# Gathering a pair of experts in two halves, with the repairs of a first neighbour

## The chip, the core and the metric

The kernel runs on one core of one Trainium2 chip. The metric is the device time of one execution, in microseconds (us). All products are on TensorE (PE); ScalarE (ACT), VectorE (DVE) and GpSimd (POOL) prepare operands and handle results, and SyncE (SP) issues the loads.

## The reference, cut to what matters

256 rows of width 1024 in fp32 go through two layers, the second with eight experts, and through a further block. What the change touches:

```python
h = h + g1 * attention(...)                                # layers 0 and 1
h = h + g2 * ffn(rms_norm(h, g) * (1 + sc2) + sh2)         # layer 0: SwiGLU; layer 1: 8 experts, top 2
# each expert: y = (silu(x @ w1) * (x @ w3)) @ w2, w1 and w3 1024x1408, w2 1408x1024

proj = rms_norm(h) @ w_in                                  # second block
qkv_a, q_c, kv_c, k_pe, gates = split(proj)                # gates = sigmoid(... + b_gate)
o_a = mixer_dilated(qkv_a, pos) @ w_o_a                    # below: a2
q, kv = rms_norm(q_c) @ w_uq, rms_norm(kv_c) @ w_ukv
o_b = mixer_mla(q, kv, rotary(k_pe), pos) @ w_o_b          # below: a3
h = h + rms_norm((g_a * o_a + g_b * o_b) @ w_out)
h = h + rms_norm(square(relu(rms_norm(h) @ w_ff1)) @ w_ff2)
```

## The kernel before, in words

**Products.** A fp32 product is three matmuls of rounded halves (`mm3`, L930 to L932): low by high, high by low, high by high. A weight tile of at most 128x2048 is loaded to `raw` by a queue of SP, ACT copies it rounded to `whi` (L1566), DVE subtracts to get `wlo` (L2133), and PE may then use it. The name of a tile's slot recurs: `whi__62` and `wlo__61` belong to `raw__60`, and so on in pairs; the same slot holds a new tile every few products.

**Order.** Each engine's program is written out by hand, one function per engine. At many places of ACT's and DVE's programs stands `feed(event)`: it converts there every tile that PE uses up to `at["ahead"]` tiles behind the tile in use at that event of PE's program. So where PE's event is placed moves the conversions in ACT's and DVE's order.

**PSUM banks.** `take(ring, ...)` gives PE the next bank of a ring and waits for what emptied that bank's last holder. Ring "8" goes round all eight banks (`turn_of["8"]` is its position), "o" is banks 6 and 7, "c" is 4 and 5, "x" is 0 to 3. Who waits for whom thus depends on the ring's position.

**Layer 0's feed-forward norm ("f").** Four row tiles are squared (`norm_square`), scaled (`norm_scale`), turned by PE (`norm_turn`) and split in halves (`norm_turned`), between tiles of the first product.

**Experts** (PE: `experts`, `hidden`, `turn_hidden`, `scatter`, `gather`). For each of eight experts: two products x by w1 and w3 in three chunks of columns (tiles of 128x2048, 128x1536 for the last chunk), each chunk turned, then the output product with w2 in six tiles, k0 = 0, 2, ..., 10 (the last of 128x1024). The scatter of expert ex-1 follows the first chunk of ex. The rows of two experts are gathered together by matmuls with a selection matrix: four turns of 128x128 ("gp", L936), then four pieces "gx" of eight matmuls (L1364), at k0 = 4 of the odd experts 1, 3 and 5. ACT and DVE scale the pieces (L1907, L2935), ACT rounds them (`pair_hi`, L1621), DVE subtracts (`moe__217`, L2205). `scattered` on DVE adds into MACC (`moe__211`, `moe__212`, L2978), for the last expert into the residual h_t (`keep__50`); the output product of that expert is multiplied by the gate row in its bank (L3013, `output_lo`) before ACT and DVE split it. POOL multiplies MACC by the gate row (L3387) and adds it to h_t (L3390), in two pairs of 128x1024 behind expert 6's scatter.

**Second block.** `norm_turn("s", 0)`, then six projections s0 to s5 and two of the latent vectors, lat0 and lat1 (`proj`, two banks each). Heads of each are turned while the next is multiplied. `gates` gives the gate projection in four parts on banks 4 and 5 (ring "c"): the first part is run at once (`advance(fill, 16)`), lat1's heads are turned, and the others fill a2's attention. Behind a2 come the products uq, ukv, their turns "mqt" (L936) and attention a3 (`attend("a3")`: scores L1182, `TENSOR_REDUCE` L2427, exponent L1645, value product L1210), in which the two tiles of the next product are converted (`at["ahead"]` is 2 from step lag + 3 on), then the output products, a norm and the MLP.

## Time and profile before

| | |
|---|---|
| median of 3 runs | 1799.89 us (1798.51 to 1800.46) |
| the profiled execution | 1800.71 us, its span 1798.5 us |
| PE busy | 1669.8 us, 93% |
| DVE busy | 1239.5 us, 69% |
| ACT busy | 832.8 us, 46% |
| POOL busy | 144.8 us, 8% |

The profiled execution is 2.2 us longer than its span, which starts with the first instruction and ends with the last; times at which something happens count from the span's start. The bracket at the end of a timeline row is the time that the engine stood idle before that instruction, and what ended it. A granted clock of 1.00 is TensorE's 2.4 GHz, 0.50 is 1.2 GHz.

### The profile page before, as it was taken

The page shows a single profiled execution, that of the slowest core. Times are in us where ns is not written, and L with a number is a line of the kernel's source. Part 1 is how long each engine was busy: PE and PEld are TensorE (multiplying, and loading weights), DVE is VectorE, ACT ScalarE, POOL GpSimd, SP SyncE. Part 2 cuts the span into 40 slices and gives each one's busy share as a digit, 9 for nine tenths or more (in the row PEclk, how much of TensorE's full clock was granted, in tenths as well). Part 3 has the DMA queues.
Part 4 walks back from the last instruction along what each step waited for, and adds up shares of the span by engine and source line. Part 5 has one row for each costly group of instructions (what it writes and reads, how often), then busy time and mean ns, then how long its engine had stood idle before and what let it go on. Part 6 is the DMA issues. An engine that isn't in the chain of part 4 may idle for free. (4 is left out here: it accounts for less than half of the span.)

```text
span 1798.5 us, 21440 instructions
## 1 busy us (share of the span) xinstructions
PE 1669.8 (93%) x8686; PEld 1423.7 (79%) x8686; DVE 1239.5 (69%) x1618; ACT 832.8 (46%) x1015; POOL 144.8 (8%) x152
## 2 busy tenths in 40 slices
PE   5999988999999998798799999999989788989998
PEld 3778877888888887797688788887779667779986
DVE  6578854587565536767689898889976465566643
ACT  6354433322122325334467677667654334545532
POOL 2110102000110022310100000000300000000000
PEclk9999989999999998998799999999999899889999
DMA  8344423355565422211479898988865422135553
GB/s 338 96 164 133 155 90 116 141 197 195 205 257 187 173 68 94 71 48 48 164 256 345 298 359 326 335 325 321 324 216 179 141 82 94 65 135 187 188 187 117
DMA packets 60504, 333.60 MB, mean 185 GB/s; under 512 B 14690, under 2 KB 15009, under 8 KB 28400
## 3 DMA queue, kind: packets, MB, share of 16 engines
q1 hardware_dynamic: 54640, 311.06, 47.6%
q0 software_dynamic: 4032, 14.57, 2.6%
q10 hardware_dynamic: 1728, 6.54, 1.0%
q8 instruction: 72, 1.18, 0.3%
q14 instruction: 32, 0.26, 0.0%
HBM read 331.00 MB, written 1.13 MB: 185 GB/s over the span
## 5 line engine op out<-in xcount | busy, mean ns | idle before, releaser
L2133 DVE TENSOR_TENSOR wlo__61<-raw__60,whi__62 128x2048 fp32r<-128x2048 f32 (+2 forms) x64 | 145.2, 2269 | 72.7 <-ACT whi__62 L1566 72.5
L2133 DVE TENSOR_TENSOR wlo__65<-raw__64,whi__66 128x2048 fp32r<-128x2048 f32 (+3 forms) x64 | 141.1, 2204 | 73.2 <-ACT whi__66 L1566 73.2
L1566 ACT ACTIVATE whi__62<-raw__60 128x2048 fp32r<-128x2048 f32 (+2 forms) x64 | 118.9, 1858 | 88.9 <-DMA raw__60<-in_ffn_w 42.4
L1566 ACT ACTIVATE whi__66<-raw__64 128x2048 fp32r<-128x2048 f32 (+3 forms) x64 | 115.3, 1802 | 82.2 <-DMA raw__64<-in_ffn_w 29.5
L2133 DVE TENSOR_TENSOR wlo__69<-raw__68,whi__70 128x2048 fp32r<-128x2048 f32 (+4 forms) x50 | 109.2, 2185 | 31.0 <-ACT whi__70 L1566 30.9
L2169 DVE SCALAR_TENSOR_TENSOR wsum__71<-raw__68,silu_rows 128x1024 f32<-128x1024 f32 x84 | 99.9, 1219 | 1.4 <-DMA raw__68<-in_ada_w 0.9
L3297 POOL TENSOR_TENSOR keep__58<-keep__58,keep__59 128x1 f32<-128x1 f32 (+3 forms) x48 | 51.6, 1079 | 593.4 <-DVE keep__58 L2210 593.3
L1566 ACT ACTIVATE whi__70<-raw__68 128x2048 fp32r<-128x2048 f32 (+4 forms) x50 | 90.4, 1808 | 15.8 <-DMA raw__68<-in_w_ff 11.6
L2133 DVE TENSOR_TENSOR wlo__235<-raw__234,whi__236 128x2048 fp32r<-128x2048 f32 (+1 forms) x24 | 50.6, 2110 | 11.8 <-ACT whi__236 L1566 11.8
L2427 DVE TENSOR_REDUCE keep__58<-ps 128x1 f32<-128x256 f32 (+1 forms) x88 | 44.5, 517 | 18.5 <-PE ps L1182 9.9
L2133 DVE TENSOR_TENSOR wlo__231<-raw__230,whi__232 128x2048 fp32r<-128x2048 f32 (+1 forms) x24 | 52.7, 2197 | 0.0
L930 PE MATMUL ps<-ffn__129,wlo__61 128*128 128x512 f32 (+1 forms) x128 | 47.7, 372 | 4.7 <-DVE ffn__130 L2205 2.9
L931 PE MATMUL ps<-ffn__130,whi__62 128*128 128x512 f32 (+1 forms) x128 | 47.1, 368 | 0.0
L932 PE MATMUL ps<-ffn__129,whi__62 128*128 128x512 f32 (+1 forms) x128 | 47.0, 367 | 0.0
L1566 ACT ACTIVATE whi__232<-raw__230 128x2048 fp32r<-128x2048 f32 (+1 forms) x24 | 42.4, 1768 | 9.6 <-DMA raw__230<-in_moe_w 9.5
L930 PE MATMUL ps<-ffn__129,wlo__141 128*128 128x512 f32 x112 | 43.6, 389 | 0.0
L931 PE MATMUL ps<-ffn__130,whi__142 128*128 128x512 f32 x112 | 43.6, 389 | 0.0
L932 PE MATMUL ps<-ffn__129,whi__142 128*128 128x512 f32 x112 | 43.6, 389 | 0.0
L930 PE MATMUL ps<-ffn__129,wlo__65 128*128 128x512 f32 x112 | 43.6, 389 | 0.0
L931 PE MATMUL ps<-ffn__130,whi__66 128*128 128x512 f32 x112 | 43.6, 389 | 0.0
L932 PE MATMUL ps<-ffn__129,whi__66 128*128 128x512 f32 x112 | 43.6, 389 | 0.0
L2169 DVE SCALAR_TENSOR_TENSOR wsum__147<-raw__144,silu_rows 128x1024 f32<-128x1024 f32 x36 | 43.2, 1220 | 0.5
(1169 smaller groups left out, 5326.9 us busy)
## 6 DMA issues: line engine op xcount, KB each, us to landing
raw__68<-in_moe_w SPq DMA_DIRECT2D x24, 1024.0 KB, 5.0
raw__60<-in_moe_w SPq DMA_DIRECT2D x24, 1024.0 KB, 5.4
raw__68<-in_ada_w SPq DMA_DIRECT2D x16, 1024.0 KB, 4.9
raw__64<-in_moe_w SPq DMA_DIRECT2D x16, 1024.0 KB, 5.2
raw__230<-in_moe_w SPq DMA_DIRECT2D x16, 1024.0 KB, 5.9
raw__234<-in_moe_w SPq DMA_DIRECT2D x16, 1024.0 KB, 6.4
raw__144<-in_ada_w SPq DMA_DIRECT2D x13, 1024.0 KB, 6.2
raw__68<-in_ada_w POOLq DMA_DIRECT2D x20, 512.0 KB, 4.1
```

The source lines that it names most:

```text
L930: e.matmul(out, ll, rh, start=start, stop=False)
L931: e.matmul(out, lh, rl, start=False, stop=False)
L932: return e.matmul(out, lh, rh, start=False, stop=stop)
L1566: e.activation(t.hi(), t.raw(), ACT.Copy).then_inc(*did("hi", i))
L2133: e.tensor_tensor(t.lo(), t.raw(), t.hi().bitcast(F32), ALU.subtract).then_inc(*did("lo", i))
L2169: m = e.scalar_tensor_tensor(out=junk, in0=slot_raw[t.slot][:, c * 1024:c * 1024 + 1024], scalar=1.0, in1=CB[:, v * D:(v + 1) * D], op0=AL ...
L2427: m = e.tensor_reduce(neg, b[:, 0:u.total], AX.X, ALU.max, negate=True)
L3297: e.tensor_tensor(x, x, EXPO[:, 0:1].broadcast_to([128, n_]) if n_ > 1 else EXPO[:, 0:1], ALU.pow).then_inc(*did(out, *key))
```

## The change

Five edits. (1) The gather of an odd expert's next pair is split: "gp" and the first two pieces stand behind k0 = 2, the other two behind k0 = 4. (2) Expert 6's output is treated as expert 7's was: multiplied by the gate row in its bank, split, and added straight into h_t; POOL's two pairs of 128x1024 become four of 128x512, released one by one by four events of experts 5 and 6. (3) In the second block ring "8" is no longer set to position 6: s0 takes banks 6 and 7 from ring "o", and the ring is moved on by two. (4) In a3 one tile is converted at step lag + 2 on ACT and lag + 4 on DVE, the other five steps later. (5) In layer 0's norm "f" one `feed` stands ahead of `norm_square(3)` on ACT and `norm_scale(3)` on DVE.

```diff
@@ -1346,3 +1346,3 @@
 
-        def gather(r, p):
+        def gather_turn(r, p):
             b = take("8", "gp", r, p)
@@ -1355,3 +1355,5 @@
             m.then_inc(*done("gp", r, p))
-            for kb in range(4):
+
+        def gather(r, p, pieces):
+            for kb in pieces:
                 b = take("8", "gx", r, p, kb)
@@ -1367,3 +1369,2 @@
                 m.then_inc(*done("gx", r, p, kb))
-            turn_of["8"] += 2
 
@@ -1410,3 +1411,5 @@
         def experts(r):
-            gather(r, 0)
+            gather_turn(r, 0)
+            gather(r, 0, range(4))
+            turn_of["8"] += 2
             for ex in range(8):
@@ -1432,6 +1435,11 @@
                     consumed(tile, "y", r, ex, k0)
-                    if k0 == 4 and ex % 2 and ex < 7:
-                        gather(r, (ex + 1) // 2)
                     if k0 == 2:
                         turn_hidden(r, ex, 2)
+                    if ex % 2 and ex < 7:
+                        if k0 == 2:
+                            gather_turn(r, (ex + 1) // 2)
+                            gather(r, (ex + 1) // 2, range(0, 2))
+                        elif k0 == 4:
+                            gather(r, (ex + 1) // 2, range(2, 4))
+                            turn_of["8"] += 2
                 if not r and ex == 1:
@@ -1468,3 +1476,2 @@
         norm_turn("s", 0)
-        turn_of["8"] += -turn_of["8"] % 8 + 6
         w_in = W["w_in_2"]
@@ -1474,3 +1481,5 @@
                 lent[slot_s] = [("scat", 1, 7, 1, 1)]
-            proj(("s", n), x4(AT2s), 2, KT, w_in[:, n * 384:(n + 1) * 384], 384, rdy("s"))
+            proj(("s", n), x4(AT2s), 2, KT, w_in[:, n * 384:(n + 1) * 384], 384, rdy("s"), "8" if n else "o")
+            if n == 0:
+                turn_of["8"] += 2
             if 0 < n < 5:
@@ -1630,5 +1639,5 @@
             A = HEADS[st]
+            if st == "a3":
+                at["ahead"] = 0
             for i in A.steps():
-                if st == "a3":
-                    at["ahead"] = 2 if i > A.lag + 2 else 0
                 if st == "a0":
@@ -1678,2 +1687,6 @@
                         e.activation(XT[1], bank("o", st, u.group), ACT.Square).then_inc(*did("hsq", "fin", u.group))
+                if st == "a3" and i - A.lag in (2, 7):
+                    at["ahead"] = 1 + (i - A.lag) // 7
+                    feed(("score", st, i, 0))
+                    at["ahead"] -= i - A.lag == 2
                 j = i - A.lag - 3
@@ -1788,3 +1801,7 @@
             norm_turned(N, 0)
-            at["ahead"] = 1 if N == "o" else 2
+            if N == "o":
+                at["ahead"] = 1
+            else:
+                at["ahead"] = 2
+                feed(("nt", N, 0, 6))
             norm_square(N, 3)
@@ -1957,3 +1974,3 @@
                 high("yph", (r, ex, half), YP[0][:, half * 512:half * 512 + 512], bank("y", r, ex, half),
-                     *([("yg", r, ex, half)] if r or ex == 7 else [("y", r, ex, 10)]), *xg_free(r, ex, "scat", 1, 1))
+                     *([("yg", r, ex, half)] if r or ex > 5 else [("y", r, ex, 10)]), *xg_free(r, ex, "scat", 1, 1))
 
@@ -2398,5 +2415,5 @@
             A = HEADS[st]
+            if st == "a3":
+                at["ahead"] = 0
             for i in A.steps():
-                if st == "a3":
-                    at["ahead"] = 2 if i > A.lag + 2 else 0
                 if st == "a0":
@@ -2466,2 +2483,6 @@
                     finished(st, A.units[j], j)
+                if st == "a3" and i - A.lag in (4, 9):
+                    at["ahead"] = 1 + (i - A.lag) // 9
+                    feed(("score", st, i, 0))
+                    at["ahead"] -= i - A.lag == 4
                 j = i - A.lag - 3
@@ -2628,2 +2649,3 @@
         at["ahead"] = 2
+        feed(("nt", "f", 0, 6))
         norm_scale("f", 3)
@@ -2940,3 +2962,3 @@
                     split_more(4, ("gx", r, p, kb))
-                for piece in (0,) if kb == 0 else (1, 2, 3):
+                for piece in ((0,), (1, 2, 3))[kb // 2] if p == 0 else (kb, kb + 1):
                     pair = slice(piece * 2, piece * 2 + 2)
@@ -2969,4 +2991,4 @@
                     past = [("acc", r, ex - 1, t, half)] if ex else [("acc", 0, 7, t, half)] if r else []
-                    past = past + ([("hpre", t)] if (r, ex) == (0, 7) else [])
-                    if r or ex == 7:
+                    past = past + ([("hpre", t, half)] if (r, ex) == (0, 6) else [])
+                    if r or ex > 5:
                         dst = h_t[t][:, half * 512:half * 512 + 512]
@@ -3008,3 +3030,3 @@
         def output_lo(r, ex):
-            for half in range(2) if r or ex == 7 else ():
+            for half in range(2) if r or ex > 5 else ():
                 for s, n in due(("y", r, ex, 10), *spr(11)):
@@ -3384,8 +3406,11 @@
         for t in range(2):
-            for s, n in due(("acc", 0, 6, t, 0), ("acc", 0, 6, t, 1), *spr(11)):
-                e.wait_ge(s, n)
-            e.tensor_tensor(MACC[t], MACC[t], GBC[:, D:2 * D], ALU.mult).then_inc(*did("hgate", t))
-            for s, n in due(("hgate", t)):
-                e.wait_ge(s, n)
-            e.tensor_tensor(h_t[t], h_t[t], MACC[t], ALU.add).then_inc(*did("hpre", t))
+            for half in range(2):
+                hs, gs = (slice(o + half * 512, o + half * 512 + 512) for o in (0, D))
+                pace = [("acc", 0, 5, 1, 1), ("hid", 0, 6, 2, 4, "3"), ("y", 0, 6, 2), ("y", 0, 6, 6)][2 * t + half]
+                for s, n in due(("acc", 0, 5, t, half), pace, *spr(11)):
+                    e.wait_ge(s, n)
+                e.tensor_tensor(MACC[t][:, hs], MACC[t][:, hs], GBC[:, gs], ALU.mult).then_inc(*did("hgate", t, half))
+                for s, n in due(("hgate", t, half)):
+                    e.wait_ge(s, n)
+                e.tensor_tensor(h_t[t][:, hs], h_t[t][:, hs], MACC[t][:, hs], ALU.add).then_inc(*did("hpre", t, half))
         for t in range(2):
```

ACT's order at the gather of expert 3, before (`whi11__236` is the tile of k0 = 8, `moe22__219` a scaled piece, `pair_hi_216` a rounded one, `whi12__240` the tile of k0 = 10):

```order
L1566 ACTIVATE whi11__236<-raw11__234 128x2048 [waits s_raw11]
L1898 ACTIVATE moe30__227<-ps3 128x512 [waits s_slot_in]
L1907 ACTIVATE moe22__219<-ps5,keep4__52 128x256 [waits s_slot_in]
L1907 ACTIVATE moe22__219<-ps5,keep4__52 128x256
L1621 ACTIVATE pair_hi_216<-moe21__218 128x512 [waits s_hid,s_moe_v]
L1621 ACTIVATE pair_hi_216<-moe22__219 128x512 [waits s_moe_a]
L1621 ACTIVATE pair_hi_216<-moe21__218 128x512 [waits s_moe_v]
L1907 ACTIVATE moe22__219<-ps7,keep4__52 128x256 [waits s_moe_v,s_slot_in]
L1907 ACTIVATE moe22__219<-ps7,keep4__52 128x256
L1621 ACTIVATE pair_hi_216<-moe22__219 128x512 [waits s_moe_a]
L1566 ACTIVATE whi12__240<-raw12__238 128x1024 [waits s_raw12]
L1566 ACTIVATE whi2__70<-raw2__68 128x2048 [waits s_raw2]
```

and in the change:

```order
L1915 ACTIVATE moe30__227<-ps3 128x512 [waits s_slot_in]
L1924 ACTIVATE moe22__219<-ps5,keep4__52 128x256 [waits s_slot_in]
L1924 ACTIVATE moe22__219<-ps5,keep4__52 128x256
L1630 ACTIVATE pair_hi_216<-moe21__218 128x512 [waits s_hid,s_moe_v]
L1630 ACTIVATE pair_hi_216<-moe22__219 128x512 [waits s_moe_a]
L1575 ACTIVATE whi11__236<-raw11__234 128x2048 [waits s_raw11]
L1630 ACTIVATE pair_hi_216<-moe21__218 128x512 [waits s_moe_v]
L1924 ACTIVATE moe22__219<-ps7,keep4__52 128x256 [waits s_slot_in]
L1924 ACTIVATE moe22__219<-ps7,keep4__52 128x256
L1630 ACTIVATE pair_hi_216<-moe22__219 128x512 [waits s_moe_a]
L1575 ACTIVATE whi12__240<-raw12__238 128x1024 [waits s_raw12]
L1575 ACTIVATE whi2__70<-raw2__68 128x2048 [waits s_raw2]
```

The tile of k0 = 8 stood ahead of all pieces, and stands between the second and the third. On DVE `wlo__235` moves in the same way, behind the second subtraction. PE's order of the pieces, and their banks, are as before.

PE at the head turns of lat0 and at the first matmul of the gates, before:

```order
L936 MATMUL ps0<-keep1__49,mix14__257 128x128 [waits s_mix_v]
L936 MATMUL ps0<-keep1__49,mix14__257 128x128 x3
L936 MATMUL ps1<-keep1__49,mix12__255 128x128 [waits s_mix_v,s_mix_a]
L936 MATMUL ps1<-keep1__49,mix12__255 128x128 x3
L930 MATMUL ps4<-whi0__62,mix20__267 128x512 [waits s_hi,s_lo,s_mix_v]
L931 MATMUL ps4<-wlo0__61,mix19__266 128x512
L932 MATMUL ps4<-whi0__62,mix19__266 128x512
```

and in the change:

```order
L936 MATMUL ps0<-keep1__49,mix14__257 128x128 [waits s_mix_v]
L936 MATMUL ps0<-keep1__49,mix14__257 128x128 x3
L936 MATMUL ps1<-keep1__49,mix12__255 128x128 [waits s_mix_v]
L936 MATMUL ps1<-keep1__49,mix12__255 128x128 x3
L930 MATMUL ps4<-whi0__62,mix20__267 128x512 [waits s_lo,s_hi]
L931 MATMUL ps4<-wlo0__61,mix19__266 128x512
L932 MATMUL ps4<-whi0__62,mix19__266 128x512
```

The gates' first bank was last held by lat1, and its matmul waited for DVE (s_mix_v) to empty it. Now lat1 is in banks 6 and 7 and lat0 in 4 and 5, and the matmul has no wait for DVE's results. In the same way uq's first matmul moves from bank 6, with a wait for s_att_v, to bank 0, without it.

DVE in a3, before (`TENSOR_REDUCE` is one step's maximum of the scores):

```order
L2462 COPY mix36__283<-ps4 128x256 [waits s_turn]
L2427 TENSOR_REDUCE keep10__58<-ps0 128x1 [waits s_score]
L2427 TENSOR_REDUCE keep10__58<-ps2 128x1 [waits s_score]
L2462 COPY mix36__283<-ps3 128x256 [waits s_pv,s_turn]
L2133 TENSOR_TENSOR wlo0__61<-raw0__60,whi0__62 128x1024 [waits s_hi]
L2133 TENSOR_TENSOR wlo1__65<-raw1__64,whi1__66 128x1024 [waits s_hi]
L2427 TENSOR_REDUCE keep10__58<-ps4 128x1 [waits s_score]
L2427 TENSOR_REDUCE keep10__58<-ps1 128x1 [waits s_score]
L2462 COPY mix36__283<-ps2 128x256 [waits s_pv,s_turn]
```

and in the change:

```order
L2479 COPY mix36__283<-ps4 128x256 [waits s_turn]
L2444 TENSOR_REDUCE keep10__58<-ps0 128x1 [waits s_score]
L2444 TENSOR_REDUCE keep10__58<-ps2 128x1 [waits s_score]
L2479 COPY mix36__283<-ps3 128x256 [waits s_pv,s_turn]
L2444 TENSOR_REDUCE keep10__58<-ps4 128x1 [waits s_score]
L2444 TENSOR_REDUCE keep10__58<-ps1 128x1 [waits s_score]
L2479 COPY mix36__283<-ps2 128x256 [waits s_pv,s_turn]
L2150 TENSOR_TENSOR wlo0__61<-raw0__60,whi0__62 128x1024 [waits s_hi]
L2444 TENSOR_REDUCE keep10__58<-ps3 128x1 [waits s_score]
L2444 TENSOR_REDUCE keep10__58<-ps0 128x1 [waits s_score]
```

Two conversions in a row stood behind two reductions of this stretch; now the first stands alone behind four, and the second (`wlo1__65`) comes eight rows further on.

## Rows read from the trace of the kernel before

**Rows 1.** PE's waits: waited for, us in total, times, longest.

```profile
PE ps L930 <- ACT moe__228 L1621: 4.0, 3, 1.3
...
PE ps L930 <- DVE wlo__239 L2133: 2.3, 3, 0.8
```

**Rows 2.** Windows: us, busy by engine, then PE's granted clock, DMA share, GB/s.

```profile
314.40:318.20 3.80, 3.73 (x18) 3.76 (x19) 0.00 (x0) 0.00 (x0) 0.00 (x0) 0.55 0.00 0
...
1415.80:1420.60 4.80, 4.71 (x11) 3.75 (x12) 2.19 (x1) 0.92 (x1) 0.00 (x0) 0.51 0.00 0
...
1508.00:1512.70 4.70, 4.69 (x15) 4.70 (x16) 1.23 (x1) 3.02 (x3) 0.00 (x0) 0.51 0.00 0
...
1538.00:1553.00 15.00, 14.73 (x63) 12.91 (x64) 5.55 (x13) 5.48 (x19) 0.00 (x0) 0.56 0.01 2
```

**Rows 3.** Timeline around the gates: start us, us, engine, line, instruction, [idle before].

```profile
1405.79 2.29 DVE L2133 TENSOR_TENSOR wlo__65<-raw__64,whi__66 128x2048 fp32r<-128x2048 f32 x1 [1.85 <-ACT whi__66 L1566]
...
1415.25 0.54 DVE L3113 TENSOR_SCALAR mix__257<-ps,keep__58 128x256 f32<-128x256 f32 x1 [0.67 <-POOL keep__58 L3297]
...
1415.89 0.76 PE L930 MATMUL ps<-whi__62,mix__267 128*128 128x512 f32 x1 [9.66 <-DVE mix__257 L3113]
...
1429.05 0.38 PE L936 MATMUL ps<-keep__49,mix__256 128*128 128x128 f32 x2
```

**Rows 4.** Timeline behind a2, DVE, PE and ACT.

```profile
1507.33 0.42 DVE L2386 TENSOR_TENSOR mix__286<-mix__286,mix__256 128x256 f32<-128x256 f32 x1
...
1508.01 0.66 PE L930 MATMUL ps<-whi__62,mix__251 128*128 128x384 f32 x1 [4.28 <-ACT mix__245 L2042]
...
1509.51 1.04 ACT L1566 ACTIVATE whi__264<-raw__262 128x1024 fp32r<-128x1024 f32 x1
```

**Rows 5.** Timeline in a3, DVE and PE.

```profile
1534.64 1.23 DVE L2133 TENSOR_TENSOR wlo__61<-raw__60,whi__62 128x1024 fp32r<-128x1024 f32 x1 [1.25 <-ACT whi__62 L1566]
...
1536.92 0.75 DVE L2427 TENSOR_REDUCE keep__58<-ps 128x1 f32<-128x256 f32 x2
...
1538.27 0.66 PE L1210 MATMUL ps<-mix__249,mix__284 128*128 128x64 f32 x4 [3.06 <-ACT mix__284 L1657]
```

**Rows 6.** Timeline in layer 0's norm, ACT and PE.

```profile
307.05 1.05 ACT L1572 ACTIVATE ffn__134<-keep__50 128x1024 f32<-128x1024 f32 x1
...
310.10 1.90 ACT L1566 ACTIVATE whi__70<-raw__68 128x2048 fp32r<-128x2048 f32 x1
...
314.47 0.46 PE L930 MATMUL ps<-ffn__129,wlo__69 128*128 128x256 f32 x1 [2.42 <-DVE wlo__69 L2133]
```

**Rows 7.** Timeline at the gather of expert 1, PE, DVE and ACT.

```profile
993.01 0.49 PE L936 MATMUL ps<-keep__49,moe__223 128*128 128x128 f32 x3
...
996.50 0.36 PE L1364 MATMUL ps<-moe__214,moe__198 128*128 128x256 f32 x1
...
998.08 0.99 DVE L2935 TENSOR_SCALAR moe__218<-ps,keep__52 128x256 f32<-128x256 f32 x2
...
1000.30 0.28 PE L1364 MATMUL ps<-moe__215,moe__199 128*128 128x256 f32 x1
...
1003.81 0.63 ACT L1621 ACTIVATE pair_hi<-moe__219 128x512 fp32r<-128x512 f32 x1
...
1009.75 0.46 PE L930 MATMUL ps<-whi__70,moe__217 128*128 128x512 f32 x1 [1.33 <-ACT moe__228 L1621]
```

**Rows 8.** Windows in experts 6 and 7.

```profile
1250.00:1275.00 25.00, 25.00 (x117) 20.83 (x117) 22.71 (x16) 19.17 (x15) 0.00 (x0) 1.00 0.98 365
...
1283.00:1303.00 20.00, 16.19 (x75) 12.81 (x74) 20.00 (x10) 10.83 (x9) 14.94 (x4) 1.00 0.75 266
```

**Rows 9.** Timeline, POOL beside DVE, and expert 6's end on DVE.

```profile
655.41 1.29 POOL L3307 TENSOR_TENSOR keep__50<-keep__50,ffn__148 128x512 f32<-128x512 f32 x1 [4.59 <-DVE ffn__148 L2476]
...
1272.12 2.29 DVE L2133 TENSOR_TENSOR wlo__65<-raw__64,whi__66 128x2048 fp32r<-128x2048 f32 x1 [0.38 <-ACT whi__66 L1566]
...
1287.50 4.49 DVE L2133 TENSOR_TENSOR wlo__61<-raw__60,whi__62 128x2048 fp32r<-128x2048 f32 x1
```

## The prediction

> **What bounds the kernel.** The shares come first: PE is busy 93% of the span, so an edit pays if it removes idle time of PE or time at which PE runs at 1.2 GHz. PE's waits by releaser tell which idle time the five edits can reach. The largest has its own row in the timeline: the gates' first matmul, 9.66 us [rows 3]. Next are uq's, 4.28 us [rows 4], a3's, 3.06 us [rows 5], the norm's, 2.42 us [rows 6], and two of about 0.8 and 1.3 us at each of the gathers of experts 1, 3 and 5, together 6.3 us [rows 1]. The windows then tell what follows such a gap: behind four of them the granted clock is about half [rows 2], while it is full in the experts [rows 8]. In a window, one minus the clock, times its length, is what 1.2 GHz cost, if PE would have been busy anyway.
>
> **Gather in two halves: +0.7 us at each of three places, +2 in all.** No matmul is added, and the matmuls of the gather were on PE's path before and stay there. What limits the next expert is the chain on ACT and DVE: last piece rounded, tile of k0 = 10 converted, then the next expert's first tile, for which PE waits until 1009.75 [rows 7] (the row names `moe__228` on ACT, but that had long been done; it is `wlo__69`). The last rounding ends at 1004.44 (1003.81 + 0.63) [rows 7]. In the change the first half follows the turn of the third chunk, which starts at 993.01 and takes 0.4 on the array; the 32 gather matmuls start 0.12 us apart (996.50 to 1000.30) [rows 7], so four turns and 16 of them take 2.4 and two pieces have left PE at 995.8. From there, an instruction that follows another starting 0.1 us before the rows' duration is over: 0.95 for scaling two half pieces, 1.1 for two roundings [rows 7], 1.8 for ACT's copy `whi__236` that now stands here [rows 6], 2.2 for `wlo__235` [rows 9], 0.95 for scaling the third piece, which waits on DVE behind that, 0.6 for its rounding, 0.95 and 0.6 for the fourth: 9.15, so 1004.95, and with semaphores between engines, of a few hundredths each, 1005.1, or 0.7 later than before. The earlier start is used up by a conversion of 4.0 us that stood ahead of the pieces and now stands between them. Behind it the chain is as before, and the next tiles are paced by DVE too, so PE doesn't get it back. Bounds: all 6.3 us of waits gone; or 1 us lost at each.
>
> **Expert 6 and the repairs: +1.7 us.** Beside POOL's four instructions PE idles 3.8 us of 20 (16.19 busy) [rows 8], since a conversion on DVE takes 4.49 us [rows 9] and not 2.29 as at 1272.12 [rows 9]. That is the gain: expert 7 has no POOL beside it, -3.8. Now the same POOL work lies in expert 6. A POOL instruction of 128x512 alone takes 1.29 us [rows 9]; I take it that each blocks one conversion for 1.15 us, half of the 2.2 us by which 4.49 exceeds 2.29. The first pair falls where DVE is well ahead and costs nothing: its cover is the slack of the tiles behind the scatter, and without it it would cost up to 2.3. The other three pairs fall into the output product: six times 1.15 is 6.9 us on DVE. To it the two multiplications of expert 6's output add 1.3, and ACT's rounding, queued behind them, delays `whi__66`, for which `wlo__65` already waited 0.38 us [rows 9]: 0.5 more. Of these 8.7 us, 2.3 fit into DVE's idle time there (22.71 busy of 25) [rows 8], while PE has none, and 0.9 into the lead that DVE has at the end of it: +5.5 for PE. Net +1.7. Bounds: nothing of it on PE, -3.8; or +4. DVE's additions for expert 6 change their target only, and POOL's last pair ends some 10 us before they need it.
> How the two engines share is a choice. I let them take turns, each POOL instruction stopping the next conversion. If both ran at half speed while both work, the same 7 us would fall on DVE sooner, some of it on tiles with less slack, and I make it +2.4; the row of 4.49 us [rows 9] fits either. The Trainium skill, page "SBUF — State Buffer", section "Who interferes with whom", speaks for turns: it calls the port pair of Vector and GpSimd an exclusive lock, which a Vector instruction with two SBUF inputs can run into. By that rule the term is +1.7, by the other reading +2.4; no row here decides.
>
> **Bank rotation: -11.7 and -6.4 us.** Nothing is added; what goes is two waits for banks. PE could begin the gates as soon as the heads of lat0 are turned, 9.66 us sooner [rows 3]. Their first tile was ready then, their second at 1408.08 (1405.79 + 2.29) [rows 3], before it is needed. The window behind the gap has clock 0.51 over 4.8 us [rows 2]: 2.35 more. Lat1's heads were turned at 1429.05 and would be at 1417.0, and DVE has them by 1415.8 (1415.25 + 0.54) [rows 3]: no new wait, but only 1.2 us to spare. I take 11.7 of the 12.0. The second wait is put down to ACT's sigmoid, but uq needs nothing of it: its bank was emptied by DVE at 1507.75 (1507.33 + 0.42) [rows 4], just before it started. So 4.28 and (1 - 0.51) x 4.7 = 2.3 go [rows 2, 4]: 6.6. Late next is ukv's tile: `whi__264` stays behind the sigmoids until 1510.55, `wlo` takes 1.2 more [rows 4, 5], so 1511.8; ukv would start at about 1512.0. I take 6.4. Bounds for both together: the gaps alone, -13.9, or less by what is given back, and -18.6.
>
> **Tiles of a3: -5.5 us.** Two conversions of 1.2 us stood ahead of a step's reduction at 1536.92, for which PE waited 3.06 us [rows 5]. With one behind two more reductions I leave a gap of 1 us: -2. The clock of 0.56 over 15 us cost 6.6 us at most [rows 2], and without the gap need not fall; but at 2.4 GHz ACT and DVE pace part of these steps, so I take 3.5, about half. Bounds: -1 (half clock comes anyway) and -8.
>
> **Norm of layer 0: -3.5 us.** ACT's copy `whi__70` stood behind square and scale of the fourth row tile, from 307.05 to 310.10 [rows 6]. First in line, it and `wlo__69` are done 3 us sooner, and PE's 2.42 us [rows 6] go with (1 - 0.55) x 3.8 = 1.7 at half clock [rows 2]: 4.1 at most. The norm's fourth tile comes 2 to 3 us later, and PE turns it some 5 us after the gap: its cover, and without it the gap would only move there. Bounds: -2 and -4.1.
>
> **Sum:** 2 + 1.7 - 18.1 - 5.5 - 3.5 = -23.4. The profiled execution took 1800.71 us (2.2 outside its span), which would become 1777.3; the median of the runs is 0.8 lower, 1799.89, so I forecast 1776.5.
>
> **Rivals.**
> (a) The gaps go and the half clock stays, or comes at other gaps close by. Then 2.35 + 2.3 + 3.5 + 1.3 = 9.4 are not gained: 1786. For it: a3 and the norm keep smaller gaps. Against: in the rows it always follows a long gap.
> (b) Gather and repairs do what one would hope: the pieces are ready early, the 6.3 us of waits go, and DVE hides the repairs (-3.8). That is 13.8 better than my sum: 1763. For it: PE delivers the first two pieces about 3 us sooner. Against: the order on ACT and the busy DVE above. Half of it, 1770, is likelier than all.
> (c) a2's steps, paced by ACT and DVE, give back the gates' gain: 1776.5 + 11.7 = 1788. For it: DVE has only 1.2 us to spare ahead of a2. Against: a2's tiles and heads were ready long before.
> (d) The change doesn't do what it says at uq: the wait really is for the sigmoid, as its row has it. Then 6.4 stay: 1783. Against: no operand or bank of uq comes from it.
> (e) Slower: turning the ring by two gives s1 to s5 the wait that the gates had, for the banks of heads not yet turned and emptied. Five such waits of 9.66 us would be 48, and 1825 the time; from 4.7 us each on, the change is slower. For it: nothing but the ring's position made the gates wait. Against: PE's order shows no new wait at these five.
>
> **From this to the numbers.** My forecast 0.52, (a) 0.15, (b) 0.17 with its half, (c) 0.07, (d) 0.05, (e) 0.02, no effect of the large edits for some cause that I don't see 0.02. The range 1766 to 1788 leaves out (e), the last, the full (b) and the ends of (a) and (c). About 0.2%, 3.6 us, is what a measurement of this kernel can tell from no change. Faster by more 0.95, within it 0.02, slower by more 0.03, where (e) is joined by the outer end of sums of bounds.
>
> **What would show it.** Right: the gates' first matmul at once behind lat0's turns, at full clock; a2's first score some 12 us sooner relative to s5; uq without a gap and ukv close behind its tile; a gap of about 1 us in a3 and clock 1.00 behind it; no wait for `wlo__69` in layer 0's norm; at three gathers the waits for `wlo__239` and the next tile a bit longer than before; PE's idle time moved from expert 7 to the end of expert 6. Wrong: the waits at the gathers shorter than before, an expert 6 without waits, half clock in a3, or a new gap in a2 of several us.

## The result, and the profile after

The change takes 1770.27 us (median of four runs, 1768.70 to 1772.38), where the kernel before took 1799.70 beside it: 0.984 of its time, interval 0.982 to 0.986, or 29.4 us less. Forecast were 1776.5 and 23.4 less; the time lies in the range.

The page of the change (busy time, share of the span, instructions; then the clock in tenths of full speed, in 40 slices):

```profile
PE 1651.8 (94%) x8686; PEld 1407.3 (80%) x8686; DVE 1236.6 (70%) x1620; ACT 831.4 (47%) x1015; POOL 155.7 (9%) x156
...
PEclk9999989999999999898889999999999999999999
```

PE has the same 8686 matmuls and is busy for 18.0 us less (1669.8 before): they run longer at 1.2 GHz, and less time is spent there. The remainder is idle time. PE's waits (us in all, times, longest):

```profile
PE ps L930 <- DVE wlo__239 L2150: 4.6, 3, 1.6
...
PE ps L930 <- DVE wlo__65 L2150: 4.4, 3, 2.9
...
PE ps L930 <- ACT moe__228 L1630: 3.9, 3, 1.3
```

The wait for `wlo__239` at the gathers has doubled, that for the next tile is as before [rows 1], and one of 2.9 us for `wlo__65` is new. Against it stand waits that are gone: the gates', uq's, the norm's and the four of expert 7; a3's is cut into smaller ones. Cut by PE's first use of a tile, the two profiled executions compare as follows (us):

| stretch | before | after | change | forecast |
|---|---|---|---|---|
| up to layer 0's norm, untouched | 304.8 | 302.0 | -2.8 | 0 |
| norm | 67.3 | 62.3 | -4.9 | -3.5 |
| up to the first split gather, untouched | 628.6 | 627.3 | -1.3 | 0 |
| three gathers and their experts | 216.6 | 218.9 | +2.4 | +2.1 |
| expert 6 and 7 | 85.8 | 86.1 | +0.3 (+5.2, -4.9) | +1.7 (+5.5, -3.8) |
| up to s5 | 37.7 | 37.2 | -0.5 | 0 |
| gates | 91.6 | 80.1 | -11.6 | -11.7 |
| a2 and uq | 82.3 | 75.7 | -6.5 | -6.4 |
| a3 | 44.8 | 37.9 | -6.8 | -5.5 |

The sum is -31.7; -27.6 of it is where the edits are or behind them, and 4.1 is in stretches whose order is unchanged. Half clock, below, is a granted clock of 0.50, 1.2 GHz.

The gates, their second head turn, the first score of a2, and uq, on PE:

```profile
1398.71 0.60 PE L936 MATMUL ps<-keep__49,mix__255 128*128 128x128 f32 x4
1399.06 0.47 PE L930 MATMUL ps<-whi__62,mix__267 128*128 128x512 f32 x1
...
1412.16 0.70 PE L1182 MATMUL ps<-mix__248,keep__50 128*128 128x256 f32 x2 [1.50 <-DVE mix__257 L3090]
...
1485.12 0.42 PE L930 MATMUL ps<-whi__62,mix__251 128*128 128x384 f32 x1
```

Of the 9.66 us [rows 3] and 4.28 us [rows 4] nothing is left; in front of a2's first score PE waits 1.50 us, where it was 1.00 before. The windows over these places, over a3 and over the norm (us, busy by engine, granted clock, DMA share, GB/s):

```profile
1399.00:1411.00 12.00, 11.66 (x55) 9.47 (x53) 9.27 (x19) 5.78 (x8) 1.10 (x2) 1.00 0.65 252
1504.00:1526.00 22.00, 19.85 (x132) 16.33 (x130) 13.17 (x30) 14.12 (x44) 0.00 (x0) 1.00 0.00 1
306.00:312.00 6.00, 6.00 (x53) 6.00 (x52) 2.36 (x2) 2.37 (x4) 0.55 (x1) 1.00 0.25 104
1485.00:1492.00 7.00, 7.00 (x43) 7.00 (x43) 3.37 (x13) 6.02 (x5) 0.00 (x0) 1.00 0.20 71
```

Where 0.51 to 0.56 stood [rows 2], the clock is 1.00. In a3 PE's waits for `mix__284` are four of 0.16, 0.34, 0.42 and 0.86 us now, where it was one of 3.06 [rows 5]. The two conversions of a3 [rows 5] on DVE, now 6.9 us apart:

```profile
1510.75 1.22 DVE L2150 TENSOR_TENSOR wlo__61<-raw__60,whi__62 128x1024 fp32r<-128x1024 f32 x1
...
1517.63 1.21 DVE L2150 TENSOR_TENSOR wlo__65<-raw__64,whi__66 128x1024 fp32r<-128x1024 f32 x1
```

In the norm, ACT's copy comes first, and PE has no gap in front of the first tile's products that use `wlo__69` [rows 6]:

```profile
304.27 1.90 ACT L1575 ACTIVATE whi__70<-raw__68 128x2048 fp32r<-128x2048 f32 x1
...
309.11 0.28 PE L930 MATMUL ps<-ffn__129,wlo__69 128*128 128x256 f32 x1
```

### The profile page after: what moved, and what is told of

It is laid out like the page before. It is cut to its first block and busy times, and to the rows that moved or that the text cites. A ratio compares the mean times of both kernels' runs of the same rounds, so it can differ in the third digit from the quotient of the medians.

```text
span 1766.6 us, 21439 instructions
## 1 busy us (share of the span) xinstructions
PE 1651.8 (94%) x8686; PEld 1407.3 (80%) x8686; DVE 1236.6 (70%) x1620; ACT 831.4 (47%) x1015; POOL 155.7 (9%) x156
## 5 line engine op out<-in xcount | busy, mean ns | idle before, releaser
L2150 DVE TENSOR_TENSOR wlo__61<-raw__60,whi__62 128x2048 fp32r<-128x2048 f32 (+2 forms) x64 | 144.2, 2253 | 72.9 <-ACT whi__62 L1575 72.7
L2186 DVE SCALAR_TENSOR_TENSOR wsum__71<-raw__68,silu_rows 128x1024 f32<-128x1024 f32 x84 | 100.0, 1221 | 1.2 <-DMA raw__68<-in_ada_w 0.6
L2150 DVE TENSOR_TENSOR wlo__239<-raw__238,whi__240 128x2048 fp32r<-128x2048 f32 (+2 forms) x24 | 43.2, 1800 | 0.9 <-ACT whi__240 L1575 0.8
```

Of the source, the lines that this page charges most:

```text
L2150: e.tensor_tensor(t.lo(), t.raw(), t.hi().bitcast(F32), ALU.subtract).then_inc(*did("lo", i))
L2186: m = e.scalar_tensor_tensor(out=junk, in0=slot_raw[t.slot][:, c * 1024:c * 1024 + 1024], scalar=1.0, in1=CB[:, v * D:(v + 1) * D], op0=AL ...
```

## The experiments

Twelve kernels were run in three sets, each beside the kernel before on the same chip (its medians were 1800.46, 1799.83 and 1799.43 us, nine runs each). `whole`, `tile_first`, `ring_only` and `old_repairs` ran on one chip, the other eight, `change_again` among them, on a second. Diffs are against the change unless another base is named. None of the kernels leaves out a part of the computation.

### The gather: what splitting it costs

**`whole`** undoes the split alone.

```diff
+                    if k0 == 4 and ex % 2 and ex < 7:
+                        gather_turn(r, (ex + 1) // 2)
+                        gather(r, (ex + 1) // 2, range(4))
+                        turn_of["8"] += 2
...
-                for piece in ((0,), (1, 2, 3))[kb // 2] if p == 0 else (kb, kb + 1):
+                for piece in (0,) if kb == 0 else (1, 2, 3):
```

> The changed kernel with its first edit undone: the gather of a pair stands whole behind k0 = 4, all else as in the change. Theory 1 (the tile of k0 = 8, converted between the two halves, delays the last piece by 0.8 us at each of three gathers): the waits ahead of the tile of k0 = 10 fall from 1.5 to 0.75 us, the three together give back 2.4 us, so 1768 where the change has 1770.3. Rival (the split saves as much elsewhere as it loses, or the delay at the gathers is made good in the next expert): 1770 within 1, or above.

It took 1768.11 us (0.983 of before, 0.982 to 0.984). PE at the first gather of this kernel:

```profile
1001.23 0.47 PE L930 MATMUL ps<-whi__240,moe__225 128*128 128x512 f32 x1 [0.77 <-DVE wlo__239 L2147]
...
1004.16 0.47 PE L930 MATMUL ps<-whi__70,moe__217 128*128 128x512 f32 x1 [1.29 <-ACT moe__228 L1627]
```

and of the change (ACT's and DVE's conversion of the tile of k0 = 8, DVE's scaling of the third piece, then PE):

```profile
988.84 1.91 ACT L1575 ACTIVATE whi__236<-raw__234 128x2048 fp32r<-128x2048 f32 x1
...
990.78 2.29 DVE L2150 TENSOR_TENSOR wlo__235<-raw__234,whi__236 128x2048 fp32r<-128x2048 f32 x1 [1.03 <-ACT whi__236 L1575]
992.99 0.99 DVE L2957 TENSOR_SCALAR moe__218<-ps,keep__52 128x256 f32<-128x256 f32 x2
...
998.57 0.47 PE L930 MATMUL ps<-whi__240,moe__225 128*128 128x512 f32 x1 [1.55 <-DVE wlo__239 L2150]
...
1001.50 0.47 PE L930 MATMUL ps<-whi__70,moe__217 128*128 128x512 f32 x1 [1.30 <-ACT moe__228 L1630]
```

The wait for `wlo__239` is 1.55 with the split and 0.77 without it; the next is the same. The rows above it show the chain of the prediction: ACT's conversion at 988.84 and DVE's at 990.78 now stand between the second and the third piece, whose scaling starts at 992.99. Each of the three gathers is some 0.77 us longer than in `whole`, 2.3 in all; +2.1 were forecast. The medians differ by 2.2 us with intervals that overlap, so it is the traces that show it: the edit that names the change slows it.

**`tile_first`** keeps the split and puts the tile of k0 = 8 ahead of the pieces again. On ACT `at["ahead"] += p > 0` stands around `feed(("gp", r, p))`; on DVE:

```diff
+                if p and kb == 0:
+                    at["ahead"] += 1
+                    feed(("gx", r, p, kb))
+                    at["ahead"] -= 1
                 for piece in ((0,), (1, 2, 3))[kb // 2] if p == 0 else (kb, kb + 1):
```

> The changed kernel, gather in two halves as there, but the tile of k0 = 8 is converted ahead: on ACT before the first piece, on DVE behind the first scaling and not behind two subtractions. Theory 1 (only the place of that conversion spoils the split): the last rounding ends some 2 us earlier, the wait for the tile of k0 = 10 goes and that for the next expert's first tile falls to about 0.6 us, 2.2 us less per gather, 6.5 in all: 1764. Rival (ACT and DVE have too much to do there in any order): within 2 us of 1770.

It took 1767.05 us (0.982, 0.980 to 0.983). The wait for `wlo__239` is gone, and of the next 0.78 is left:

```profile
1001.72 0.48 PE L930 MATMUL ps<-whi__70,moe__217 128*128 128x512 f32 x1 [0.78 <-ACT moe__228 L1630]
```

Each gather is 1.8 us and then 0.54 us shorter than in the change, 7.0 in all, and 4.7 shorter than unsplit. So the split pays once the conversion is out of the pieces' way. The median is only 3.2 us below the change's, between the two theories. The profiled execution of this kernel has three spells of half clock that the change's has not: behind the 2.93 us wait of expert 6 (1.6 us), one more between expert 7 and s5 (1.4), and one at the end of a3 (1.6). At the last two places this kernel and the change are the same.

### The banks

**`ring_only`** is the kernel before with edit 3 alone.

```diff
-        turn_of["8"] += -turn_of["8"] % 8 + 6
...
-            proj(("s", n), x4(AT2s), 2, KT, w_in[:, n * 384:(n + 1) * 384], 384, rdy("s"))
+            proj(("s", n), x4(AT2s), 2, KT, w_in[:, n * 384:(n + 1) * 384], 384, rdy("s"), "8" if n else "o")
+            if n == 0:
+                turn_of["8"] += 2
```

> The kernel before with the third edit alone, the position of ring 8 in the second block. Theory 1 (two waits for banks and the half clock behind them): 18.4 us less than before, 11.9 at the gates and 6.5 at uq, so 1781. Rival (a third of it comes from the other edits, or a2 gives some back when its tiles are not late): 1785 or more.

1781.76 us (0.991, 0.989 to 0.992), 18.7 below before. The gates' first matmul stands right behind lat0's turns:

```profile
1403.13 0.60 PE L936 MATMUL ps<-keep__49,mix__255 128*128 128x128 f32 x4
1403.49 0.48 PE L930 MATMUL ps<-whi__62,mix__267 128*128 128x512 f32 x1
```

Gates and uq gain 10.14 and 1.91, 4.67 and 1.94 us (gap and half clock of each); 0.4 of it is given back later in the gates. No projection from s1 to s5 has a new wait. This settles what the wait of 9.66 us was: nothing had to be ready for the gates that wasn't, only the bank was held. And the sigmoid, which the trace names as uq's releaser, released nothing: without a change to it, the wait is gone.

### Expert 6, expert 7 and the repairs

**`old_repairs`** undoes edit 2: expert 6 goes through MACC, and POOL works in two pairs of 128x1024 behind its scatter, in expert 7 (the diff is that of edit 2, reversed).

> The changed kernel with its second edit undone: POOL's two pairs of 128x1024 behind the scatter of expert 6, no gate row on expert 6's output. Theory 1 (the same POOL work stretches conversions in expert 7, 3.8 us of waits there, and the 5.2 us lost in expert 6 are not): expert 6 free of waits, 3.8 us in expert 7, in sum 1 us faster to 1 us slower than the change, 1769 to 1771. Rival (moving the repairs is worth its 3.8 us, expert 6's waits have another cause): 1773 or more.

1771.23 us (0.984, 0.983 to 0.986), 1.0 more than the change, which the intervals don't separate. Expert 6 has no wait, and expert 7 has its four:

```profile
1288.62 0.47 PE L930 MATMUL ps<-whi__62,moe__217 128*128 128x512 f32 x1 [1.36 <-DVE wlo__61 L2150]
...
1296.36 0.41 PE L930 MATMUL ps<-whi__232,moe__217 128*128 128x384 f32 x1 [1.54 <-DVE wlo__231 L2150]
```

(The other two are 0.39 and 0.53 us.)

From PE's first use of `whi__236` in expert 6 (at 1226.24 in the change) to its first use in expert 7 it takes 49.13 us here and 54.31 in the change, +5.2; from there to its use in expert 7's third chunk 20.68 and 15.86, -4.8. The work is moved and its cost with it: +0.4 in the trace.

Where expert 6 loses it, in the change (POOL, DVE, PE):

```profile
1228.48 8.81 POOL L3412 TENSOR_TENSOR moe__211<-moe__211,keep__57 128x512 f32<-128x512 f32 x1 [355.78 <-DVE moe__212 L3000]
...
1228.31 2.29 DVE L2150 TENSOR_TENSOR wlo__69<-raw__68,whi__70 128x2048 fp32r<-128x2048 f32 x1
1230.51 2.29 DVE L2150 TENSOR_TENSOR wlo__61<-raw__60,whi__62 128x2048 fp32r<-128x2048 f32 x1
1232.71 1.76 DVE L2150 TENSOR_TENSOR wlo__65<-raw__64,whi__66 128x1536 fp32r<-128x1536 f32 x1
1234.38 1.75 DVE L2150 TENSOR_TENSOR wlo__231<-raw__230,whi__232 128x1536 fp32r<-128x1536 f32 x1
...
1260.29 3.39 DVE L2150 TENSOR_TENSOR wlo__69<-raw__68,whi__70 128x2048 fp32r<-128x2048 f32 x1
...
1266.89 1.28 DVE L3035 TENSOR_TENSOR ps<-ps,keep__57 128x512 f32<-128x512 f32 x2
...
1270.64 2.29 DVE L2150 TENSOR_TENSOR wlo__65<-raw__64,whi__66 128x2048 fp32r<-128x2048 f32 x1 [1.11 <-ACT whi__66 L1575]
...
1263.82 0.47 PE L930 MATMUL ps<-whi__70,moe__217 128*128 128x512 f32 x1 [1.25 <-DVE wlo__69 L2150]
...
1273.08 0.47 PE L930 MATMUL ps<-whi__66,moe__217 128*128 128x512 f32 x1 [2.92 <-DVE wlo__65 L2150]
```

PE has three waits: 1.25 and (not shown) 0.26 us behind conversions stretched to 3.39 and 3.37, and 2.92 us for `wlo__65`, which waits on DVE for ACT's `whi__66`, itself behind the roundings of the output that DVE multiplies at 1266.89. The first of POOL's eight instructions took 8.81 us: it ended at 1237.29, 1.16 us behind the end of the fourth conversion (1234.38 + 1.75), about the time that it takes alone; none of these four conversions took longer than usual.

**`unpaced`** (on `tile_first`) releases POOL's four pairs together.

```diff
-                pace = [("acc", 0, 5, 1, 1), ("hid", 0, 6, 2, 4, "3"), ("y", 0, 6, 2), ("y", 0, 6, 6)][2 * t + half]
+                pace = ("acc", 0, 5, 1, 1)
```

> As tile_first, but all of POOL's four pairs wait only for expert 5's last addition, so that they run one behind the other. Theory 1 (POOL and DVE take turns, each POOL instruction stops the next conversion by 1.15 us wherever conversions follow each other): the first multiplication again waits 7.5 us for four conversions in a row, the others stop conversions between 1235 and 1250, 3 to 4 us of waits there, none of 1.2 us at the end of the output product; 1767 to 1769. Rival (DVE keeps the port as long as its conversions follow each other, as at the first multiplication): POOL finishes late, PE loses next to nothing, 1765 or less.

1763.84 us (0.980, 0.979 to 0.982). That is the rival's time, but not by its mechanism: POOL is done 25 us behind its start, not 36 as in the change, and PE waits for the conversions that it stretches.

```profile
1222.33 8.82 POOL L3418 TENSOR_TENSOR moe__211<-moe__211,keep__57 128x512 f32<-128x512 f32 x1 [348.84 <-DVE moe__212 L3006]
...
1222.18 2.28 DVE L2152 TENSOR_TENSOR wlo__69<-raw__68,whi__70 128x2048 fp32r<-128x2048 f32 x1
...
1266.68 0.47 PE L930 MATMUL ps<-whi__66,moe__217 128*128 128x512 f32 x1 [1.71 <-DVE wlo__65 L2152]
```

The first multiplication again waits out four conversions, the next three instructions take 1.28 to 1.31 us where DVE converts nothing, and the last four stretch four conversions. PE loses 0.81, 0.41, 0.46 and 0.30 us there, but 1.71 instead of 1.22 + 0.27 + 2.93 at the end. Counted by when PE's matmuls arrive, the waits are only 0.2 us shorter than in `tile_first` (4.9 and 5.1 us); what `unpaced` gains in its trace is half clock that doesn't come, 1.6 us behind the last wait and 1.2 before s5.

**`tiles_first`** (on `tile_first`) converts two tiles ahead of expert 6's output, on ACT and on DVE.

```diff
+                at["ahead"] += 2 * (not r and ex == 6)
                 feed(("y", r, ex, 10))
+                at["ahead"] -= 2 * (not r and ex == 6)
```

> As tile_first, and the two tiles of expert 7's first chunk that stood behind expert 6's output are converted ahead of its multiplication and rounding, on ACT and DVE. Theory 1 (the 2.9 us wait is for a tile that stands behind yg, yph and ypl): that wait goes, and the half clock of 1.3 us behind it; the scatter of expert 6 still comes in time: 4.2 less than tile_first, 1763. Rival (DVE is the bound there whatever the order): the wait moves to a later tile or to the scatter, within 1 us of tile_first.

1766.12 us (0.981, 0.980 to 0.983), 0.9 less than `tile_first`, which the intervals don't separate. The wait of 2.93 us goes (3.1 us, and 1.6 of half clock), and 2.0 of it comes back in expert 7, which finds its output later:

```profile
1280.42 0.47 PE L930 MATMUL ps<-whi__70,moe__217 128*128 128x512 f32 x1 [1.79 <-DVE wlo__69 L2154]
```

**`at_once`** (on `unpaced`) lets each pair start as soon as its own addition is done.

```diff
-                for s, n in due(("acc", 0, 5, t, half), pace, *spr(11)):
+                for s, n in due(("acc", 0, 5, t, half), *spr(11)):
```

> As unpaced, but each of POOL's pairs waits only for its own addition of expert 5, so the first multiplication starts while DVE still adds from PSUM. Theory 1 (the port goes to whoever is there first; in turns once one of them has been stopped): the first multiplication takes 1.3 to 1.5 us instead of 8.8, the next POOL instructions stop conversions at once, from the first behind the additions, 1.1 us each, while DVE has 1 to 2 us in hand there; PE waits 1 to 2 us before 1235; 1764 to 1766. Rival (at the first conversions of that stretch DVE keeps the port anyway): a POOL instruction of 8 us again, same time as unpaced.

1764.27 us (0.980, 0.979 to 0.982), as `unpaced`.

```profile
1224.46 1.31 POOL L3417 TENSOR_TENSOR moe__211<-moe__211,keep__57 128x512 f32<-128x512 f32 x1 [347.05 <-DVE moe__211 L3006]
...
1224.95 1.40 DVE L3006 SCALAR_TENSOR_TENSOR moe__212<-ps,moe__201,moe__212 128x512 f32<-128x512 f32 x2
1226.27 3.02 DVE L2152 TENSOR_TENSOR wlo__69<-raw__68,whi__70 128x2048 fp32r<-128x2048 f32 x1
1229.21 3.37 DVE L2152 TENSOR_TENSOR wlo__61<-raw__60,whi__62 128x2048 fp32r<-128x2048 f32 x1
...
1269.63 0.47 PE L930 MATMUL ps<-whi__66,moe__217 128*128 128x512 f32 x1 [1.10 <-DVE wlo__65 L2152]
```

POOL now starts beside DVE's additions from PSUM (L3006), which keep their 1.40 us, as POOL keeps its 1.31. So the 8.81 us are not the price of the first instruction: where they come, POOL's instruction arrives just behind the start of a conversion, and others are queued behind it. Here POOL is already running when the first conversion comes, each takes its turn, and the conversions take 3.02, 3.37, 2.84 and 2.84 instead of 2.28, 2.28, 1.75 and 1.75. PE doesn't wait for these, which have slack, against the 1 to 2 us of waits that were expected before 1235; it waits 0.52, 0.41 and 0.46 us for later ones, and the last wait is 1.10.

**`both`** joins `unpaced` and `tiles_first`.

> unpaced and tiles_first in one kernel. Theory 1 (the two are independent: unpaced's remaining wait of 1.7 us is for the tile behind expert 6's output, and DVE has nearly 2 us more in hand there than in tiles_first, so the wait does not come back in expert 7): 1.9 less than unpaced, 1762. Rival (it comes back as in tiles_first, 1.8 us at expert 7's next chunk): 1764.

1763.36 us (0.981, 0.979 to 0.982). The wait of 1.71 is gone, one of 0.56 for `wlo__69` comes in expert 7: 1.1 us net in the trace, 0.5 in the medians, which does not separate it from `unpaced`.

**`both_k10`** also converts the tile of k0 = 10 ahead of the third piece.

```diff
+                at["ahead"] += p > 0 and kb > 1
                 feed(("gx", r, p, kb))
+                at["ahead"] -= p > 0 and kb > 1
...
-                if p and kb == 0:
+                if p:
```

> As both, and at the three gathers the tile of k0 = 10 is converted ahead of the third piece's rounding on ACT (idle 2.4 us there) and of its subtraction on DVE. Theory 1 (the last 0.8 us of wait at each gather is for the next expert's first tile, which stands behind the tile of k0 = 10 on ACT): the three waits go, 3 us less than both, 1759. Rival (DVE is full there): the wait stays within 0.3 us, 1762.

1761.58 us (0.979, 0.978 to 0.981), the lowest median of the study (its interval overlaps those of `both` and `unpaced`) and 13.3 below the change in the same set. No gather has a wait any more, 0.95 us less at each. Half of these 2.9 us is hidden in the profiled execution by a spell of half clock at the end of a3 (1.5 us) that `both` has not. PE's first and last wait between 985 and 1305 us:

```profile
1235.96 0.42 PE L930 MATMUL ps<-whi__236,moe__217 128*128 128x384 f32 x1 [0.81 <-DVE wlo__235 L2156]
...
1277.23 0.47 PE L930 MATMUL ps<-whi__70,moe__217 128*128 128x512 f32 x1 [0.20 <-DVE wlo__69 L2156]
```

with three more of 0.42, 0.47 and 0.30 between them, where POOL's last four instructions stretch the conversions.

### a3 and the norm

**`a3_pair`** undoes edit 4, on ACT and on DVE, and both tiles are converted in a row again.

```diff
-            if st == "a3":
-                at["ahead"] = 0
             for i in A.steps():
+                if st == "a3":
+                    at["ahead"] = 2 if i > A.lag + 2 else 0
...
-                if st == "a3" and i - A.lag in (2, 7):
```

> The changed kernel with its fourth edit undone: both tiles are converted together in a3 from step lag + 3 on. Theory 1 (the pair costs a gap of 3.1 us, and the half clock behind it some 3.7 more): a3 takes 6.8 us more than in the change, 1777. Rival (the gap alone, the clock falls only because uq's gap came shortly before it): 3 us more and clock 1.00 behind it, 1773.

1782.53 us (0.990, 0.989 to 0.992). PE's wait and the window behind it:

```profile
1518.92 1.12 PE L1210 MATMUL ps<-mix__249,mix__284 128*128 128x64 f32 x4 [3.03 <-ACT mix__284 L1666]
```

```profile
1518.00:1532.00 14.00, 13.08 (x50) 11.36 (x50) 4.82 (x12) 4.93 (x18) 0.00 (x0) 0.52 0.00 1
```

uq has no gap in this kernel, and a3 is at half clock all the same. a3's own gap brings it, then, and not a state that uq's gap left behind. The stretch is 7.6 us longer than in the change. The median is 12.3 higher than that of the change's first runs, but 7.7 higher than that of `change_again`, which ran on the same chip (below).

a3 has another spell of half clock that the change's profile doesn't show. At its end PE waits 1.02 us (`mix__256`), in every kernel alike; the first window behind that wait is of the change, the second of `tile_first`:

```profile
1526.70:1530.70 4.00, 3.95 (x20) 3.32 (x21) 1.51 (x2) 3.25 (x3) 0.00 (x0) 1.00 0.00 0
```

```profile
1524.60:1528.60 4.00, 3.92 (x13) 3.31 (x14) 1.06 (x3) 2.76 (x3) 0.00 (x0) 0.57 0.00 0
```

PE's waits ahead of it are the same to 0.01 us. Of the eleven profiled executions with edit 4, four have the spell (`tile_first`, `tiles_first`, `norm_first`, `both_k10`), and it costs them 1.5 to 1.6 us. So what edit 4 gains is 6.8 us in some executions and some 5.3 in others.

**`norm_first`** undoes edit 5.

```diff
                 at["ahead"] = 2
-                feed(("nt", N, 0, 6))
...
         at["ahead"] = 2
-        feed(("nt", "f", 0, 6))
```

> The changed kernel with its fifth edit undone: in layer 0's norm ACT squares and scales the fourth row tile ahead of the tile's conversion. Theory 1: a gap of 2.4 us at the tile, 1.7 at half clock behind it, and a second stretch of half clock some 12 us later that the trace of before has and that of the change has not: 4.9 us more, 1775. Rival (4.1 as the rows of before priced it, the rest was drift): 1774.

1778.96 us (0.988, 0.987 to 0.990). PE's wait and the window:

```profile
312.48 0.35 PE L930 MATMUL ps<-ffn__129,wlo__69 128*128 128x256 f32 x1 [2.42 <-DVE wlo__69 L2149]
```

```profile
312.40:316.40 4.00, 3.92 (x22) 3.95 (x23) 0.00 (x0) 0.00 (x0) 0.00 (x0) 0.64 0.00 0
```

The norm is 4.1 us longer than with the edit, 2.57 in the gap and 1.56 behind it, as the rival had it; so is the median against that of `change_again`, on the same chip. The half clock of the kernel before had a second spell in the norm in its profile, which isn't there in this one: it was no part of what the edit removes.

### The change once more

**`change_again`** is the change, unaltered, in the last set.

> The change itself once more, for the scatter between runs: 1770 within 2, and in its trace the edited stretches take what they took in the first one (gathers +0.8 us each, gates -11.9, uq -6.5, a3 -6.8, norm -4.1 or -5), while the stretch up to 300 us, which no edit touches, may differ by 1 to 3 us. Rival: the edited stretches scatter as much.

1774.86 us (0.987, 0.985 to 0.989): 4.6 above the first set, outside its interval. The edited stretches repeat within 0.1 us (gathers +0.81, +0.79, +0.79; expert 7 -1.61, -0.63, -1.77, -0.75; gates -10.14, -1.92; uq -4.66, -1.94; a3 -6.85), but for two. The norm gains 4.6 us, not 4.9. And the same wait of 2.94 us in expert 6 is followed by a lower clock here,

```profile
1274.00:1284.00 10.00, 8.42 (x31) 6.83 (x32) 9.26 (x6) 8.57 (x6) 0.00 (x0) 0.83 0.57 186
```

and in the first profiled execution it is not:

```profile
1271.00:1281.00 10.00, 7.92 (x34) 6.50 (x35) 10.00 (x7) 9.87 (x7) 0.00 (x0) 1.00 0.74 234
```

That is 1.3 us. Another 1.5 come between expert 7 and s5, where the clock falls twice and not once; the remainder is spread over untouched stretches, as the 4.1 us of the first comparison were. So a difference of a few us between medians of different sets says little, and the sizes of the edits are better read from the stretches.

## Why the prediction was right, and where its sizes were off

The sum of its steps was -23.4. The medians give -29.4 in the first comparison and -24.6 in the last set, the edited stretches of the first pair of traces -27.6, with 4.1 more where no edit is. So between 1 and 6 us were missed, and part of it is scatter that no step could have had.

- **Gather, +2.1: right**, +2.4, and for the reason given. The chain was worked out 0.7 us longer, and 0.79 was measured.
- **Expert 6 and the repairs, +1.7: measured +0.3 to +0.4.** The gain in expert 7 was taken as PE's idle time, 3.8; the matmuls arrive 4.8 to 4.9 us sooner. The bracket of a wait leaves out about 0.23 us each time: the four of expert 7 were 1.36, 0.39, 1.54 and 0.53, the delays behind them 1.61, 0.63, 1.77 and 0.75. The loss in expert 6, +5.5, was 5.2, but its make-up was otherwise, and that the sum came close is in part luck. Half of 2.2 us is 1.1, not 1.15. "Six times 1.15" us of stretched conversions, 6.9, were 4.8 us in all, in five conversions (`wlo__65` at 3.23, `wlo__235` at 2.90, `wlo__69` at 3.39, `wlo__61` at 3.37 instead of 2.29, and the smaller `wlo__239` at 2.31 instead of 1.22), since not every POOL instruction stops one for its whole time; the wait for `whi__66` was 1.11 and not 0.38 + 0.5. That the first pair costs nothing was right, though not by the slack: it stopped no conversion.
- **How POOL and DVE share: turns, as assumed.** A stretched conversion takes 3.37 us, 1.1 more than 2.29: about what POOL's instruction takes alone (1.29). At half speed, with POOL's instructions one behind the other as in `at_once`, it would take 4.6, twice 2.29. And beside the 8.81 us of the first multiplication four conversions keep their length, which sharing would not leave them. The Trainium skill, page "SBUF — State Buffer", section "Who interferes with whom", describes this as an exclusive lock on the port pair of the two engines. The runs agree with it, with 3.37 us; how long a turn can be made to wait (8.81 us) it doesn't tell.
- **Banks, -18.1: right**, -18.1 in the change's trace, -18.7 in `ring_only`'s median. The choice to give uq's wait to the bank, against the row's own label, held.
- **a3, -5.5: mis-sized**, -6.8 in the change, 7.6 by undoing it. The step that failed is "so I take 3.5, about half" of the half clock's 6.6 us. PE's waits in the steps went from 3.06 to 1.78 us in four, 1.3 less where 2 was put, with none above 0.86 (a gap of 1 us had been named); so 5.5 us of the 6.8 came from the clock, where 3.5 was put. (In the four kernels with the spell at the end of a3 1.5 to 1.6 of it are lost again.) At full speed ACT and DVE hold these steps up far less than assumed.
- **Norm, -3.5: mis-sized**, 4.1 by undoing it and -4.9 in the first comparison. Against the 2.42 us wait stands a later arrival of 2.57. The 0.6 that was kept back from the 4.1 was not needed.
- **Rivals.** (a) fell for the change, in both its profiles: no half clock at any of the four places; `a3_pair` shows that it follows a3's own gap. Its second half, half clock at a smaller wait close by, came true at the end of a3 in four of the other kernels. (b) fell: the waits at the gathers grew. That its halved form gave 1770, the time measured, is luck: the 6 us come from a3, expert 6 and the norm and from untouched stretches. What it hoped for is there to be had, as `tile_first` (4.7 us better than unsplit) and `both_k10` (no wait left) show; the place of the tiles in the change prevents it. (c) fell but for a trace: in front of a2's first score PE waits 0.5 us longer than before, of a gain of 12.1. (d) and (e) fell with `ring_only`.

## What to carry to other kernels

A wait for a ring's next bank can be a large false wait, here 9.66 us and 4.28: when PE stands idle and its operands are ready, look who last held the bank, and shift the ring before touching the work. When an operation is moved earlier in a hand-written order, look at what is issued with it on the other engines: here the split gather lost 0.8 us each time to a weight conversion that slipped between its pieces, and gained 1.6 us over the unsplit one once that stood in front. Moving POOL's work to another stage moved its cost along (5.2 us lost, 4.8 gained); it cost nothing where DVE worked from PSUM or PE had tiles in hand. And a difference of a few us between two kernels that stall is not yet a gain: look first whether the clock fell behind the same wait in the one and not in the other.

## What the runs showed of the hardware

- **POOL beside DVE.** Conversions with both operands in SBUF and POOL's additions in SBUF take turns of whole instructions (2.29 becomes 3.37); additions of DVE with an operand in PSUM and POOL's don't disturb each other (1.40 and 1.31 in `at_once`). A POOL instruction that arrived 0.15 to 0.17 us behind the start of a conversion, with three more queued, was done only after the fourth: 8.81 us in the change, 8.82 in `unpaced`. The change's third multiplication came 0.08 us behind the start of a conversion with a subtraction from PSUM queued behind it, and was done after that one conversion, in 3.36 us. What decides when its turn comes is open; no run varied this alone.
- **The clock after a short gap.** Gaps of 3.03 us (a3) and 2.42 us (norm) were followed by half clock, 0.52 over 14 us and 0.64 over 4 us. The same gap of 2.9 us in expert 6 was followed by it in three kernels and in the repeat of the change, at a cost of 1.3 to 1.6 us, and not in `whole` nor in the change's first profile (clock 0.79 to 0.82 over 8 us in the one case, 1.00 in the other). Two waits as short as 0.86 and 1.02 us, 4.4 us apart at the end of a3, were followed by a clock of 0.57 over 4 us in four kernels, and by 1.00 in seven with the same waits. What tells them apart was not found.
